# Rounded part and remainder of each weight side by side in one buffer, in a one-core hybrid attention layer

## The reference, cut to what matters

```python
xn = rmsnorm(h, norm_g)
aq, ak, av, agate, iq, ik, iw, cq, ckv, kr, bgate, mg = split_proj(xn @ w_in)   # 2048 x 9872
o_a = dsa_attend(...)                       # indexer, top-k, grouped attention
y_a = (o_a * silu(agate)) @ w_o_a           # 1024 x 2048
cq  = rmsnorm(cq, q_norm_g);   qb = cq @ w_uq      # 512 x 1536
ckv = rmsnorm(ckv, kv_norm_g)
k_nope = ckv @ w_uk;  v = ckv @ w_uv        # 512 x 1024 each
o_b = mla_attend(...)
y_b = (o_b * silu(bgate)) @ w_o_b           # 1024 x 2048
g = sigmoid(mg)
h = h + (g[..., :D] * y_a + g[..., D:] * y_b) @ w_out     # 2048 x 2048
y = rmsnorm(h, final_g)
```

## Time and profile before

| | |
|---|---|
| median of 2 runs | 918.9 us (918.8 to 919.01) |
| span of the profiled execution | 914.2 us |
| TensorE busy | 883.3 us (97%), 6398 matmuls |
| weight loads busy (they overlap the matmuls) | 856.1 us (94%) |
| VectorE busy | 494.1 us (54%) |
| ScalarE busy | 352.3 us (39%) |
| GpSimd busy | 20.7 us (2%) |
| share of the chain that ended last | PE 94%, DVE 3%, ACT 1%, DMA 1%, issue 1% |

### The profile page before, as it was taken

One profiled execution on the slowest core, in us unless ns is written; L12 is line 12 of the kernel. 1 busy time (PEld: TensorE's weight loads), 2 busy tenths in 40 slices (PEclk: granted clock), 3 DMA queues, 4 the chain that ended last, 5 costly groups with the idle time before them and its releaser, 6 DMA issues.

```text
span 914.2 us, 15326 instructions
## 1 busy us (share of the span) xinstructions
PE 883.3 (97%) x6398; PEld 856.1 (94%) x6398; DVE 494.1 (54%) x728; ACT 352.3 (39%) x451; POOL 20.7 (2%) x40
## 2 busy tenths in 40 slices
PE   4999999999999999999999999999999999999993
PEld 3899988999999999879999999999999999999993
DVE  4365685667986644244554343345556566644453
ACT  4333443434354555123334333243433323333542
POOL 3010000200000000000000000000000000000000
PEclk9999999999999999999999999999999999999997
DMA  9455422544454244212335555454555545584502
GB/s 302 143 173 180 143 92 93 187 152 155 139 166 127 76 168 138 92 47 92 108 94 169 162 159 177 145 184 145 176 161 162 179 148 173 187 291 152 171 0 103
DMA packets 123646, 135.08 MB, mean 148 GB/s; under 512 B 2592, under 2 KB 119376, under 8 KB 122896
## 3 DMA queue, kind: packets, MB, share of 16 engines
q1 hardware_dynamic: 121712, 127.41, 44.4%
q0 software_dynamic: 1888, 7.01, 2.2%
HBM read 130.72 MB, written 3.69 MB: 147 GB/s over the span
## 4 chain that ended last, share of the span: by engine, by line
PE 94%; DVE 3%; ACT 1%; DMA 1%; issue 1%; SPq 0%; DVEq 0%; ACTq 0%; PEldq 0%
PE ps L439 27%; PE ps L441 27%; PE ps L440 26%; PE ps L499 2%; PE ps L550 2%; PE ps L645 2%; PE ps L720 1%; DVE w_lo L1340 1%; PE ps L722 1%; PE ps L721 1%; ACT w_hi L803 1%; DMA x_tok<-in_x_prompt 1%; PE ps L612 1%; PE ps L624 1%; PE ps L613 1%; PE ps L778 1%
## 5 line engine op out<-in xcount | busy, mean ns | idle before, releaser
L439 PE MATMUL ps<-x_hi,w_hi 128*128 128x288 f32 x1504 | 453.3, 301 | 0.5 <-DVE w_lo L1340 0.5
L440 PE MATMUL ps<-x_lo,w_hi 128*128 128x288 f32 x1504 | 445.5, 296 | 0.0
L441 PE MATMUL ps<-x_hi,w_lo 128*128 128x288 f32 x1504 | 444.3, 295 | 0.0
L1105 DVE TENSOR_TENSOR w_lo<-raw,w_hi 128x2048 fp32r<-128x2048 f32 (+1 forms) x102 | 232.8, 2282 | 264.5 <-ACT w_hi L803 263.5
L803 ACT CAST w_hi<-raw 128x2048 fp32r<-128x2048 f32 (+1 forms) x118 | 223.6, 1895 | 389.2 <-PE ps L441 358.3
L439 PEld LDWEIGHTS ps<-x_hi,w_hi 128*128 128x128 f32 x1504 | 283.9, 189 | 4.3 <-issue 3.0
L441 PEld LDWEIGHTS ps<-x_hi,w_lo 128*128 128x128 f32 x1504 | 284.9, 189 | 0.0
L440 PEld LDWEIGHTS ps<-x_lo,w_hi 128*128 128x128 f32 x1504 | 284.4, 189 | 0.1
L441 PE MATMUL ps<-og_hi,w_lo 128*128 128x288 f32 x256 | 75.9, 296 | 0.0
L439 PE MATMUL ps<-og_hi,w_hi 128*128 128x288 f32 x256 | 75.7, 296 | 0.0
L440 PE MATMUL ps<-og_lo,w_hi 128*128 128x288 f32 x256 | 74.6, 292 | 0.0
(11 more groups left out here) (215 smaller groups left out, 725.9 us busy)
## 6 DMA issues: line engine op xcount, KB each, us to landing
raw<-in_w_in SPq DMA_DIRECT2D x76, 1024.0 KB, 5.2
raw<-in_w_out SPq DMA_DIRECT2D x16, 1024.0 KB, 5.5
raw<-in_w_o_a SPq DMA_DIRECT2D x8, 1024.0 KB, 5.4
raw<-in_w_o_b SPq DMA_DIRECT2D x8, 1024.0 KB, 5.4
raw<-in_w_uq SPq DMA_DIRECT2D x4, 768.0 KB, 4.5
x_tok<-in_x_prompt SPq DMA_DIRECT2D x2, 1024.0 KB, 6.7
raw<-in_w_in SPq DMA_DIRECT2D x4, 512.0 KB, 10.3
raw<-in_w_uk SPq DMA_DIRECT2D x2, 1024.0 KB, 5.1
```

The source lines that it names most:

```text
L439: nc.tensor.matmul(out, hi, x_h, start=first, stop=False)
L440: nc.tensor.matmul(out, hi, x_l, start=False, stop=False)
L441: return nc.tensor.matmul(out, lo, x_h, start=False, stop=last)
L1105: nc.vector.tensor_tensor(w_lo[:, step % 2, 0:n], raw[:, step % RAW, 0:n], w_hi[:, step % 2, 0:n].bitcast(F32), ALU.subtract).then_inc(lo_ ...
```

## The change

Two buffers become one. `w_hl` is [128, 2, 4096]; in each slot the elements alternate: rounded part of column 0, remainder of column 0, rounded part of column 1, and so on. `w_hi` and `w_lo` become views of it that take every second element, at a distance of 8 bytes instead of 4. The total size is the same. Nothing else in the program is edited: the same instructions run in the same order on every engine with the same waits, and only the addresses of the operands that are weights differ.

```diff
-        (x_hi, x_lo, raw, w_hi, w_lo, ident, ones, rope_tab, norm_g, lora_g, ss, var, root, rstd,
+        (x_hi, x_lo, raw, w_hl, ident, ones, rope_tab, norm_g, lora_g, ss, var, root, rstd,
          mx, neg_mx, sum_p, inv_p, o_base) = row(
             -(-nc.sbuf_base // 64) * 64,
             ("x_hi", [P, KD, NTOK], F32R), ("x_lo", [P, KD, NTOK], F32R), ("raw", [P, RAW, 2048]),
-            ("w_hi", [P, 2, 2048], F32R), ("w_lo", [P, 2, 2048], F32R), ("ident_sb", [P, P]), ("ones", [P, P]),
+            ("w_hl", [P, 2, 4096], F32R), ("ident_sb", [P, P]), ("ones", [P, P]),
...
+        w_hi, w_lo = (w_hl[:].rearrange("p s (n two) -> p s n two", two=2)[:, :, :, part] for part in range(2))
```

## The result

| | before | after |
|---|---|---|
| median | 918.9 us | 947.24 us (947.11 to 947.37, 2 runs) |
| span of the profiled execution | 914.2 us | 945.3 us |

The ratio after to before is 1.0352 (95% interval 1.0309 to 1.0395). The change makes the kernel slower by 28 us; the two spans differ by 31.

What follows compares the result with a forecast made beforehand. TensorE, busy for 97% of the span, was taken as the bound. The 914.2 us span plus 27.2 (a) and 0 for (b, c, d) gave 941.4; with 4.7 us outside the span, 946.1 us, 3.0% slower, range 916 to 985.

Steps and rivals of the forecast that it cites:

- (a): Moving weights of the value projection: price per column doubles, 0.227 us more on each of 120 matmuls, 27.2 us.
- nothing slows: Rival: an 8-byte step is free for the value projection's moving stream too, giving 919 us; chance 0.31.
- The rule on cachelines: Skill page rule: full rate with two consecutive accesses per 16-byte line, so no engine slows at 8-byte steps.
- The reason given for (a): At 0.44 ns per element the moving stream reads SBUF fastest, so suffers first when half the bytes fetched are unused.
- (b): Stationary weight loads, 5616 blocks of 128 columns: at most 0.110 us each, hidden under matmuls of 0.133; no cost.
- The worry about the cover: Loads have only 0.023 us of cover, called the thinnest, being taken from transposes whose operands are not strided.
- The bound of 0.110 us from the transposes: Transposes, each loading a 128x128 block, start 0.110 us apart, so a weight load takes at most that.
- (c): ScalarE's cast writing w_hi with stride: doubled it is +1.78 us per step; taken at no cost.
- (d): VectorE's subtraction reading w_hi and writing w_lo with stride: doubled it is +2.14 us per step; taken at no cost.
- The rule on adjacent pairs: Skill page rule: ports need adjacent 4-byte word pairs; hopping costs 1.7 to 2.5 times, VectorE near (d) doubled.
- that rival: ScalarE and VectorE slow in the splits: 935 us at +25%, about 1166 us if both double; chance 0.13.
- The signs: Profile checks: L720 to L722 about 0.46 us apart, 753 matmuls in 500 to 600 us, cast 1.91, subtraction 2.29 us.

Runs made afterwards that it cites:

- e1_only_uv: Kernel before with only the two steps of w_uv stored alternately, the other 116 steps contiguous: 940.54 us against 913.43, ratio 1.0299.
- e4_latents: Kernel before with weights as they were, but the activations of the latent projections alternating element by element: 953.42 us against 913.43, ratio 1.0452.
- e3_uv_pairs: Kernel before with only the w_uv steps stored in alternating runs of two rounded parts and two remainders: 940.4 us.
- h0: Kernel before, contiguous weights, each merge projection matmul cut into two of 144 columns with a load each: 980.9 us, one run.
- h1: Merge projection matmuls cut in two as in h0, with weights outside w_uv stored alternately at 8-byte steps: 1000.0 us, one run.
- e2_all_but_uv: Kernel before with all steps stored alternately except the two of w_uv: 919.64 us against 913.43, ratio 1.0077.

## Why the prediction was right, and where it was not

Forecast 946 us, measured 947.24.

**What bounds the kernel, and (a).** Right. The 120 moving matmuls were to go from 0.232 to 0.46 us and to add 27.2 us; the profile shows 0.453 and 26.6, in a stage of 54.6 us where 55 were forecast, and the value projection alone gives +27.1 us (e1_only_uv). That the cost is the moving role is shown by the activations (e4_latents). The lower bound, which was the rival "nothing slows" with a chance of 0.31, is excluded. The rule on cachelines of the Trainium skill ("SBUF — State Buffer", section on DMA ports, note on cachelines), by which two accesses per line are enough for the full rate, is not borne out for this operand: 0.453 us with two per line, also where the two are adjacent (e3_uv_pairs, 0.454). For loads, cast and subtraction it held to within 9% at 8 bytes.

**The reason given for (a)** was only half right. "Half the bytes fetched are unused" predicts more for three unused quarters; the 16-byte step shows 0.461 us. It is a fall to half pace, and it depends on whole aligned lines. The speed of the stream did point to the right one of the four accesses, but no run shows that the speed is why.

**(b) The loads.** Taken at nothing with a cover of 0.023 us. The load rose by 0.008 us (h0, h1), inside the cover, and still the pace rose: by 0.7 ns a matmul in 600 to 700 us, some 3.4 us over the 4848 matmuls concerned outside the branch outputs, and by 2.6 us over the 768 of the branch outputs. The step that failed is "before TensorE saw anything": a load that is shorter than the matmul above it was not free to the last nanosecond. By what path it costs, and why most in the branch outputs, is open. The worry about the cover was in place: at 16 bytes it is gone, and the kernel takes 1659 us. The bound of 0.110 us from the transposes came out (0.111 in h0), but they could not show it: their 128 plain f32 columns alone take 0.108 us at the pace of L570, so the distance need not be the load's.

**(c) The cast.** Taken at nothing, measured +0.16 us (+9%). The chain that ended last holds five casts before, at 1.80 to 1.91 us, and the same five after at 1.96 to 2.08: 0.8 us. Two more come onto it after, at 213.59 and 224.14 us, before attention A. So (c) gives about 1 us, and (b) and (c) about 7, against +6.2 us measured together (e2_all_but_uv).

**(d) The subtraction.** Nothing, right: 2.294 us. The rule on adjacent pairs of the Trainium skill ("Vector Engine (DVE) Microarchitecture Reference", section 5.2), by which VectorE would have slowed, is not borne out here at a step of 8 bytes. At 16 bytes the price is 1.7 times the contiguous one, near what its table gives for hops. The prediction read that table a little high: it has 1.71 to 2.51 ns per column against 1.054, which is 1.6 to 2.4 times and not 1.7 to 2.5. Nor would VectorE alone at its doubled price have reached the upper end of that rival: 2.14 us a step are just over the 2.1 that are free, so some 38 us, about 957.

**The signs.** Two that the prediction named came out against it: the cast at 2.075 us instead of 1.91, and the stretch of 500 to 600 us, where 753 matmuls were to stay. There are 744 in it, in part because the stages lie later; e2_all_but_uv, whose stages do not, has 749. By its own words the prediction is wrong there, in (b) and (c).

**The sum.** It came within 1.1 us of the median, but not for the stated reasons alone. Beside the experiments the whole effect is 33 us, 27 for (a) and 6 for (b) and (c), which the sum left out. The two first profiles differ by 31.1 us, and the rows above account for it: 26.6 (a), 6.0 (b), about 1 (c) and 1.7 for the second fall of the clock, less 3.6 for the shorter start at half pace, together 31.7. The medians differ by 28. The kernel before was measured at 918.9 us for the prediction and at 913 to 914 beside the experiments. So the prediction was right in cause and in the large term and short by 6 us, and the total came nearer than its terms by luck.

## What to carry to other kernels

Ask of every layout change which role an operand plays on TensorE. A moving fp32r operand keeps full pace only in whole 16-byte lines, here from aligned runs of four elements on; a stationary one, a cast or a subtraction can be read or written at every second element for 0 to 9% more, but at every fourth for 1.7 to 2.1 times the price. Where a few matmuls stream what all others load, as the value projection does here, check these few first: 2% of the matmuls carried four fifths of the loss.

## What the hardware showed that was not expected

- Runs of four elements on 16 bytes stream as fast as a contiguous row (0.233 us for 512 columns), and 8 bytes of misalignment cost a factor of two (0.453).
- The moving stream does not get slower from a step of 8 to one of 16 bytes (0.453, 0.461), while a load does (0.119, 0.234).
- In the kernel with the 16-byte step the granted clock is at its lower level, 0.50, from 742 to 1104 us, in the cut merge projection, with matmuls of 144 columns waiting for loads of 0.234 us; among the matmuls of 288 columns that follow it is at 1.00. The count of matmuls in 100 us hardly differs (427 and 430): with the loads as the limit the clock of the array did not matter. The busy times by stretch of that kernel, the granted clock in the third column from the end:

```profile
900.00:1000.00 100.00, 100.00 (x427) 100.00 (x427) 19.75 (x5) 17.26 (x7) 0.00 (x0) 0.50 0.17 52
1200.00:1300.00 100.00, 100.00 (x430) 100.00 (x430) 44.89 (x23) 39.55 (x18) 0.00 (x0) 1.00 0.30 92
```
